# Keeping the masked backward scores: one value product per block on the sum of both directions, added on GpSimd

## What is computed

```python
def chunked_gated_recurrence(q, k, v, log_f):
    '''S_t = diag(f_t) S_{t-1} + k_t v_t^T, o_t = S_t^T q_t, in chunkwise form.'''
    ...
    scores = jnp.einsum('bhncd,bhnsd->bhncs', q_dec, k_intra)
    scores = jnp.where(tri_mask, scores, 0.0)
    o_intra = jnp.einsum('bhncs,bhnse->bhnce', scores, v)
    ...
    o = o_intra + jnp.moveaxis(o_inter, 0, 2)

o_fwd = chunked_gated_recurrence(q, k_f, v, g_f)
o_bwd = rev(chunked_gated_recurrence(rev(q), rev(k_b), rev(v), rev(g_b)))
o = o_fwd + o_bwd
```

## Time and profile before

| | |
|---|---|
| median of 3 runs | 1699.22 us (1698.62 to 1700.44) |
| the profiled execution, its own time | 1699.87 us |
| its span, first to last instruction | 1698.2 us |
| PE busy | 1592.7 us (94%) |
| DVE, ACT, POOL busy | 537.3, 396.1, 167.6 us |
| recurrence (240 to 795 us of the span): PE busy | 539.48 of 555 us |

### The profile page before, as it was taken

The page is one execution under the profiler, slowest core; times in us unless marked ns, Lnnn a source line. Parts: engine busy times, 40 slices in busy tenths (PEclk is TensorE's granted clock), DMA queues, the critical chain, the costliest instruction groups (busy, mean ns, idle before and its releaser), DMA issues.

```text
span 1698.2 us, 20396 instructions
## 1 busy us (share of the span) xinstructions
PE 1592.7 (94%) x7532; PEld 794.9 (47%) x7532; DVE 537.3 (32%) x1115; ACT 396.1 (23%) x578; POOL 167.6 (10%) x230
## 2 busy tenths in 40 slices
PE   7999999999989989998938999999999999999990
PEld 3444455546545545544524444444444444444440
DVE  3840055344525535444561111111111111111114
ACT  4120154354355342214411000000000000000004
POOL 2010000000000000010010111111100111111100
PEclk9999999999999999999968999999999999999995
DMA  5131142142132333445838788888988999888848
GB/s 217 45 117 64 71 138 75 51 143 84 54 103 79 125 124 134 156 149 197 310 139 347 272 335 334 335 332 336 333 333 335 340 346 339 334 331 332 331 150 309
DMA packets 76851, 368.43 MB, mean 217 GB/s; under 512 B 9072, under 2 KB 21872, under 8 KB 63600
## 3 DMA queue, kind: packets, MB, share of 16 engines
q1 hardware_dynamic: 57488, 300.90, 46.2%
q0 software_dynamic: 18720, 65.02, 12.5%
q10 hardware_dynamic: 576, 1.59, 0.2%
HBM read 301.42 MB, written 66.06 MB: 216 GB/s over the span
## 4 chain that ended last, share of the span: by engine, by line
PE 53%; issue 6%; ACT 1%; DMA 1%; DVE 1%; POOL 0%; DVEq 0%; POOLq 0%; ACTq 0%
PE bank L1742 28%; PE bank L1766 14%; PE bank L1591 7%; PE bank L1735 2%; PE bank L1757 1%; ACT junk L959 1%; PE bank L1537 0%; DMA x_dram<-mid,sidx 0%; POOL early L713 0%; PE bank L1546 0%; DMA wup<-x_dram 0%; PE bank L1563 0%; PE bank L1562 0%; DMA mid<-xn_dram,gidx 0%; PE bank L1523 0%
## 5 line engine op out<-in xcount | busy, mean ns | idle before, releaser
L1742 PE MATMUL bank<-wup,xgT 128*128 128x512 f32 x1088 | 480.6, 595 | 1.4 <-ACT xgT L939 1.4
L1445 PE MATMUL bank<-wide,mid 128*128 128x512 f32 x960 | 423.8, 597 | 3.5 <-issue 3.5
L1742 PEld LDWEIGHTS bank<-wup,xgT 128*128 128x128 f32 x1088 | 204.7, 191 | 246.5 <-issue 244.4
L1445 PEld LDWEIGHTS bank<-wide,mid 128*128 128x128 f32 x960 | 180.2, 191 | 218.3 <-issue 217.3
L1766 PE MATMUL bank<-wide,hidT 128*128 128x512 f32 x544 | 240.9, 596 | 4.2 <-DVE hidT L1415 4.2
L1766 PEld LDWEIGHTS bank<-wide,hidT 128*128 128x128 f32 x544 | 101.3, 191 | 119.3 <-issue 119.3
L1591 PE MATMUL bank<-early,mid 128*128 128x512 f32 x288 | 127.3, 596 | 0.0
L946 ACT ACTIVATE sil<-bank 128x512 f32<-128x512 f32 x34 | 20.3, 597 | 435.0 <-PE bank L1742 435.0
L1388 DVE TENSOR_SCALAR mid<-bank,gate_of 128x512 f32<-128x512 f32 x68 | 51.1, 751 | 212.2 <-PE bank L1766 212.2
L735 POOL DMA_INDIRECT x_dram<-mid,sidx x34 | 53.6, 1577 | 644.0 <-DVE mid L1388 297.4
L939 ACT ACTIVATE xgT<-bank 128x512 f32<-128x512 f32 x70 | 38.1, 595 | 275.1 <-PE bank L1735 275.1
(11 more groups left out here) (214 smaller groups left out, 1313.7 us busy)
## 6 DMA issues: line engine op xcount, KB each, us to landing
wup<-w SPq DMA_DIRECT2D x68, 2048.0 KB, 16.0
wide<-w SPq DMA_DIRECT2D x34, 2048.0 KB, 9.4
u_dram<-ustage POOLq DMA_DIRECT2D x60, 256.0 KB, 2.4
rin<-u_dram SPq DMA_DIRECT2D x60, 256.0 KB, 4.2
mid<-w_in SPq DMA_DIRECT2D x23, 512.0 KB, 3.5
wide<-x_t SPq DMA_DIRECT2D x12, 512.0 KB, 11.3
mix_dram<-mixst POOLq DMA_DIRECT2D x24, 256.0 KB, 2.5
mid<-x_all SPq DMA_DIRECT2D x12, 512.0 KB, 5.5
```

Of the source, the lines that this page charges most:

```text
L1445: last = pe.matmul(PROJ[u % 3][:, :], wsec[:, slot, k, :], nT[:, k, g * GT:(g + 1) * GT], start=(k == 0), stop=(k == KT - 1))
L1742: last = pe.matmul(bank[out_bank][:, :], xgT[:, k, :], weights[:, s, k, :], start=(k == 0), stop=(k == KT - 1))
```

## The change

The masked scores of a backward step now go to their own blocks of `scb`, a tile that holds all 12 blocks of the head, and stay there. Those of a forward step go to `scf`. In a forward step POOL adds `scf` and the 4 blocks of `scb` of the same group into `scsum`, and PE multiplies the values by that sum. In a backward step PE multiplies only the states. `scsum` lies in the tile of `wpool`, and `zeros` is now a part of `scb`; DVE waits for the two transfers from `zeros` (`tails_zeroed`) before it clears the bank SC, and so before anything is written to `scb`.

```diff
-        scT = [sb(mixing, f"scT{d}", [P, BG, P]) for d in (FWD, BWD)]
+        scf = sb(mixing, "scf", [P, BG, P])
+        scb = sb(mixing, "scb", [P, NT, P])
...
-        zeros = sb(mixing, "zeros", [P, D])
+        scsum = wpool
+        zeros = scb[:, :, :].rearrange("p b c -> p (b c)")[:, 0:D]
...
-            pool.memset(zeros[:, :], 0.0)
-            for d in (FWD, BWD):
-                made(pool.memset(scT[d][:, :, :], 0.0))
+            made(pool.memset(scb[:, :, :], 0.0))
+            made(pool.memset(scf[:, :, :], 0.0))
...
+            def sum_scores(h, n):
+
+                d, g = STEPS[n]
+                if d == FWD:
+                    pool.wait_ge(st_ready, h * NS + (n + 1))
+                    pool.wait_ge(o_ready, h * NS + n)
+                    pool.tensor_tensor(scsum[:, :, :], scf[:, :, :], scb[:, g * BG:(g + 1) * BG, :],
+                                       ALU.add).then_inc(scsum_ready, 1)
+
...
                 for n, (d, g) in enumerate(STEPS):
+                    sum_scores(h, n)
                     if more:
                         store_unit(h + 1, BEFORE + PER_STEP * n)
...
             dve.wait_ge(consts_ready, CONSTS)
+            dve.wait_ge(tails_zeroed, 32)
             dve.memset(SC[:, :], 0.0)
...
-                dve.copy_predicated(scT[d][:, :, :], tri[d][:, :].bitcast(u32).unsqueeze(1).to_broadcast([P, BG, P]),
+                kept = scf[:, :, :] if d == FWD else scb[:, g * BG:(g + 1) * BG, :]
+                dve.copy_predicated(kept, tri[d][:, :].bitcast(u32).unsqueeze(1).to_broadcast([P, BG, P]),
                                     SC[:, :].rearrange("p (b c) -> p b c", c=P)).then_inc(st_ready, 1)
...
+                if d == FWD:
+                    pe.wait_ge(scsum_ready, h * NG + (g + 1))
                 for b in range(BG):
                     cs = slice(b * P, (b + 1) * P)
-                    pe.matmul(OUT[:, cs], vtok[:, g * BG + b, :], scT[d][:, b, :], start=True, stop=False)
+                    if d == FWD:
+                        pe.matmul(OUT[:, cs], vtok[:, g * BG + b, :], scsum[:, b, :], start=True, stop=False)
                     last = pe.matmul(OUT[:, cs], state[:, b if d == FWD else b + 1, :], qint[:, cs],
-                                     start=False, stop=True)
+                                     start=(d == BWD), stop=True)
```

More of the change, by code:

```diff
@@ L290, in trunk_program @@
         st_ready = sem("st_ready")
+        scsum_ready = sem("scsum_ready")
         o_ready = sem("o_ready")
```

## The result

The changed kernel takes 1688.79 us (median of 4, 1687.52 to 1689.55), the kernel before beside it 1699.51 us (median of 4): a ratio of 0.9936, with a 95% interval of 0.9919 to 0.9953. It is 10.7 us faster; 1688.5 us was forecast.

The account below looks back on a forecast made before the run. PE, busy for 1592.7 us of the span, was taken to bound the kernel. Backward steps -10.7 us, the sum on POOL 0 and the rest 0 gave a median of 1688.5 us, range 1685.5 to 1692.0.

Parts of the forecast that it names:

- The price of a product: Backward steps on PE: 4 products, 8 records of 0.112 us, go from each; 12 x 0.895 = 10.7 us saved.
- rival b: Backward steps on PE: the state's products alone are bound by weight loads, only 3 us saved, 1696.2 us; 4 in 100.
- The path: Backward steps: PE runs without waits between products and the transposes' input is ready early, so the saved time counts in full.
- Rival (c): Whole kernel: no change, 1699.2 us, since DVE's or a transfer's chain sets the steps; 3 in 100.
- The keys' lead over their transposes: Backward step: `kst` ended 6.0 us before its transposes began; about 5 us of this would be left.
- The sum on POOL: Forward steps: 12 sums of 128x512 on POOL, 1.2 us each, at most 2.7, hidden before PE's outputs; cost 0.
- the bound of 1.6: Forward steps: up to 1.6 us added to DVE's queries and keys beside POOL's sum; cost 0.
- The slack: Forward steps: from the mask's end to PE's outputs 9.6 us, 7.0 us in the narrowest, head 3's last.
- Rival (d): Forward steps: the sum comes too late and PE waits in all; slower, 1702.6 us at x = 10.6; 2 in 100.
- 12x - 112.6: Forward steps: cost in us of sums ending x us after the mask; eats the gain at x = 10.3.
- Rival (a): PE after idle time: one low-clock stretch of 2.2 us more or less, 1690.7 or 1686.3 us; two more, 6 in 100.
- PE's busy time in the recurrence down by nearly 11 us: Sign expected in the profile after: PE busy for nearly 11 us less in the recurrence, from 539.48 us before.

Follow-up runs that it names:

- The unused sums: Changed kernel, but each step multiplies the values by its own scores; POOL still makes all 12 sums and PE waits for them, unread: 1699.53 us, ratio 0.9999 to the kernel before.
- the repeated sums: Changed kernel with each POOL sum made 4, 6 or 8 times in a row, PE waiting for the last: 1687.31, 1690.86 and 1723.88 us.
- the 8 sums: Changed kernel with each POOL sum made 8 times in a row, PE waiting for the last: 1723.88 us, ratio 1.0141 to the kernel before.

## Why the prediction was right

- **The price of a product.** 0.895 us per backward step was forecast; steps became 0.89 us shorter. Adding, moving and removing the products gave the same price in every step. That the state's products could be bound by their weight loads (rival b) is excluded by the 0.90 us of eight records.
- **The path.** PE sets every step: forward steps without their products shrink too. Rival (c) falls with it. The keys' lead over their transposes, 6.0 us in the step of the earlier trace rows, is 5.1 there now, where about 5 was forecast.
- **The sum on POOL.** 1.2 us was forecast; 1.26 alone, 1.6 beside DVE. It began 0.08 us after the mask. The rise of DVE's next instruction was 0.95 us, under the bound of 1.6. The unused sums put the price of all of it at 0, within 1.5 us. The taking of turns at a shared pair of ports, which the prediction cited from the Trainium skill (SBUF — State Buffer, "SBUF: two separate sides"), fits these rows: the first instruction of DVE, under way, kept its 0.68 us, and the next waited. The prediction's estimate of 1.1 us, from a figure of the Trainium skill (GPSIMD Engine Reference, "Performance versus the Vector engine"), was a little low against the 1.26 measured alone.
- **The slack.** 7.0 us at the narrowest was read off from two rows, and the repeated sums confirm it: no wait with 4 of them, waits in the narrow steps alone with 6. Rival (d), a loss, needs more than six. Its formula, 12x - 112.6, took 9.6 us of slack for eleven steps. In fact these leads run from 8.3 to 17.3, and the formula left out the low-clock time behind waits.
- **What was less good than it looks.** The total agreed to 0.3 us, and part of that is luck: the recurrence gave 10.0 us of the 10.7 forecast, and the other parts, which moved by up to 2.2 us in both directions, happened to add most of the rest. Rival (a) is not one event of 2.2 us, as it was put, but a smaller scatter at several places: the same 48 records took 22.4 to 23.9 us behind the stall in the ten kernels that kept it (before, after, and all experiments up to the 8 sums). "PE's busy time in the recurrence down by nearly 11 us" was 9.8 for that reason (522.33 to 512.50).

## What to carry to other kernels

Where one engine is busy without a break, count its products in distances from start to start, and look for sums that can be made before a product instead of after it: two products with the same weights become one, and the addition goes to any engine whose result is needed late enough. Read the slack off the rows (end of the input, start of the user) before choosing the engine, and test it by repeating the work. An experiment that changes values in a kernel with data-dependent routing must be compared by stages, or made so that the values stay.

## What the runs showed of the hardware

A tensor-tensor of 128x512 on POOL takes 1.26 us alone (4 of 12) and 1.5 to 1.6 us when an instruction of DVE with two operands in SBUF has just begun (8 of 12); DVE's next then takes 1.64 us instead of 0.69. So side by side the addition costs DVE 0.95 us, more than the 0.69 us of making it there itself.

PE's stall at the branch of its loop was 2.65 to 4.47 us with the product for the squares, and PE's wait for them, ahead of the branch, and 1.0 to 1.1 us with that product behind it. In the first case it ends 7.9 to 8.3 us after the last outputs of head 1 began, whatever their number; in the second, 3.0 us after. In both it ends 1.6 to 1.8 us after a transfer of 16 KB on the instruction queue. That agrees with the fetching of the loop's instructions as the cause, but no run changed the fetching by itself, so the cause stays open.
